# Late gates in the places of k, q and v, and the heads' outputs split early, in a two-block transformer kernel on one core

## The reference

```python
proj = xn @ w_in[i]
q, k, v, u, gates = jnp.split(proj, splits, axis=-1)
...
q = rope(rmsnorm(q, q_norm_gain[i]), cos, sin)
k = rope(rmsnorm(k, k_norm_gain[i]), cos, sin)
...
o = diff_attention(q, k, v, lam)      # 8 heads of 2 x 64, values of 128: (p0 - lam * p1) @ v
o = rmsnorm(o, subln_gain[i]) * (1.0 - lam_init)
attn_branch = o.reshape(bsz, seq, V_COLS) @ w_attn_proj[i]
s = s5_layer(u, ...)
ssm_branch = s @ w_ssm_proj[i]
g_attn, g_ssm = jnp.split(jax.nn.sigmoid(gates), 2, axis=-1)
h = h + (g_attn * attn_branch + g_ssm * ssm_branch) @ w_out[i]
```

## Time and profile before

| | us |
|---|---|
| median of 3 runs | 1477.43 (1476.66 to 1480.17) |
| the profiled execution, its own time | 1480.89 |
| its span, first to last instruction | 1479.1 |
| PE busy | 1414.4 (96%) |
| ACT busy | 829.7 (56%) |
| DVE busy | 658.1 (44%) |
| POOL busy | 203.6 (14%) |
| mean granted clock of PE | 0.988 |

### The profile page before, as it was taken

The page is one execution under the profiler, slowest core; times in us unless marked ns, Lnnn a source line. Parts: engine busy times, 40 slices in busy tenths (PEclk is TensorE's granted clock), DMA queues, the critical chain, the costliest instruction groups (busy, mean ns, idle before and its releaser), DMA issues.

```text
span 1479.1 us, 18389 instructions
## 1 busy us (share of the span) xinstructions
PE 1414.4 (96%) x6786; PEld 1120.0 (76%) x6786; DVE 658.1 (44%) x1153; ACT 829.7 (56%) x1159; POOL 203.6 (14%) x235
## 2 busy tenths in 40 slices
PE   3999999999899999999999999899999999999994
PEld 2887777677578878888888877677788888888883
DVE  4884345465533445555135154746555211212124
ACT  4644666676564566565455376555766655535431
POOL 0120110010011111111111111110111111111111
PEclk9999999999999999999999999999999999999997
DMA  8889876556359878888978997554576888887971
GB/s 256 192 177 185 206 163 145 130 125 150 93 116 245 194 172 198 188 190 192 217 167 196 216 227 172 128 140 113 130 173 141 191 198 188 197 204 176 205 151 57
DMA packets 80675, 255.34 MB, mean 173 GB/s; under 512 B 16592, under 2 KB 17744, under 8 KB 80464
## 3 DMA queue, kind: packets, MB, share of 16 engines
q0 software_dynamic: 32544, 118.50, 44.3%
q1 hardware_dynamic: 47616, 132.57, 29.4%
q10 hardware_dynamic: 432, 3.15, 0.6%
HBM read 128.09 MB, written 3.41 MB: 89 GB/s over the span
## 4 chain that ended last, share of the span: by engine, by line
PE 88%; DVE 4%; ACT 4%; DMA 2%; issue 1%; SPq 1%; POOLq 0%; POOL 0%; DVEq 0%; ACTq 0%
PE pg L500 26%; PE pg L502 25%; PE pg L501 25%; PE ps L637 2%; PE py L701 1%; DMA toep<-k_dram 1%; PE ps L799 1%; PE px L654 1%; PE ps L809 1%; DMA w_lo<-w_raw 1%; DMA w_raw<-weights 1%; PE px L532 1%; PE py L819 1%; ACT w_lo L901 0%; PE px L534 0%
## 5 line engine op out<-in xcount | busy, mean ns | idle before, releaser
L500 PE MATMUL pg<-x_hi,w_hi 128*128 128x512 f32 x1168 | 469.0, 402 | 10.7 <-DVE x_lo L1319 9.9
L502 PE MATMUL pg<-x_hi,w_lo 128*128 128x512 f32 x1168 | 457.8, 392 | 0.0
L501 PE MATMUL pg<-x_lo,w_hi 128*128 128x512 f32 x1168 | 457.6, 392 | 0.0
L468 POOL DMA_DIRECT2D w_lo<-w_raw x226 | 194.8, 862 | 1235.4 <-ACT w_lo L901 1209.1
L900 ACT ACTIVATE w_hi<-w_raw 128x1024 fp32r<-128x1024 f32 x226 | 237.6, 1051 | 123.8 <-PE pg L502 107.1
L500 PEld LDWEIGHTS pg<-x_hi,w_hi 128*128 128x128 f32 x1168 | 221.3, 189 | 64.2 <-issue 13.8
L501 PEld LDWEIGHTS pg<-x_lo,w_hi 128*128 128x128 f32 x1168 | 221.3, 189 | 47.5 <-issue 3.4
L502 PEld LDWEIGHTS pg<-x_hi,w_lo 128*128 128x128 f32 x1168 | 220.9, 189 | 47.2
L901 ACT ACTIVATE w_lo<-w_raw 128x1024 fp32r<-128x1024 f32 x226 | 236.4, 1046 | 0.0
L500 PE MATMUL pg<-act_hi,w_hi 128*128 128x512 f32 x432 | 168.0, 389 | 0.0
L501 PE MATMUL pg<-act_lo,w_hi 128*128 128x512 f32 x432 | 168.0, 389 | 0.0
(11 more groups left out here) (278 smaller groups left out, 1523.3 us busy)
## 6 DMA issues: line engine op xcount, KB each, us to landing
w_raw<-weights SPq DMA_DIRECT2D x226, 512.0 KB, 4.6
w_lo<-w_raw POOLq DMA_DIRECT2D x226, 512.0 KB, 5.7
kq_rot<-kq_raw SPq DMA_DIRECT2D x64, 64.0 KB, 2.4
hid<-x SPq DMA_DIRECT2D x4, 512.0 KB, 5.7
hid<-x ACTq DMA_DIRECT2D x1, 2048.0 KB, 11.0
out<-hid SPq DMA_DIRECT2D x8, 256.0 KB, 2.0
u_dram<-hid SPq DMA_DIRECT2D x4, 256.0 KB, 7.0
pairs<-u_dram SPq DMA_DIRECT2D x8, 128.0 KB, 7.4
```

The lines of the kernel that those rows point to most:

```text
L468: pool.dma_start(w_lo[:, s], w_raw[:, s], accum_op=ALU.add).then_inc(lo_in[s], 16)
L500: pe.matmul(bank[:], wh, xh(k), start=n == 0, stop=False)
L501: pe.matmul(bank[:], wh, xl(k), start=False, stop=False)
L502: last = pe.matmul(bank[:], wl, xh(k), start=False, stop=n == len(ks) - 1)
```

## The change

The late gates move: in iteration 8 gate 4 takes the place of k, gate 5 that of q, gate 6 that of v; in iteration 9 gate 7 takes that of k. Their order, and so the order of the weight units, is unchanged. On ACT each `late_gate` moves with its tile; it is also the call that splits the weights three units on.

The heads' outputs no longer go to `x_hi` and `x_lo`. A new buffer `o_split` of 15 tiles lies over the buffers of rope, k, q and v, a sixteenth tile `pairs_r[:, 2]` over `sqr[:, 0]`; each head gets two of these that no longer hold anything in use. `o_high` (ACT) and `o_low` (DVE) split heads 0 and 1 in iteration 8 behind `turned`, 2 to 4 at its end, 5 and 6 in iteration 9 ahead of the reads of pv 7, and 7 behind the loop. The sum of squares of head 7 (`o_sums`) moves from the end of iteration 9 into attn 0, ahead of its step k = 2. Attn reads the new buffers. `mix_hi` and half of `mix_lo` move on to the buffers of values and probabilities, the other half to that of `y5`.

```diff
@@ -196,6 +196,8 @@
         hid = sb("hid", [P, KT, T])
+        with ExitStack() as s:
+            pairs_r = sb("pairs_r", [P, 4, T], F32R, scope=s)
         pairs = sb("pairs", [P, 4, T])
@@ -214,6 +216,8 @@
             gates = sb("gates", [P, 16, T], scope=first)
+            with ExitStack() as s:
+                mix_lo_high = sb("mix_lo_high", [P, 4, T], F32R, scope=s)
             y5 = sb("y5", [P, SSM_T, T], scope=first)
@@ -241,8 +245,9 @@
                 pt = sb("pt", [P, QB, T], scope=s)
+            o_split = sb("o_split", [P, 15, T], F32R, scope=first)
             mix_hi = sb("mix_hi", [P, KT, T], F32R, scope=first)
-            mix_lo = sb("mix_lo", [P, KT, T], F32R, scope=first)
+            mix_lo_low = sb("mix_lo_low", [P, 4, T], F32R, scope=first)
@@ -301,6 +306,18 @@
         k_dram = nc.dram_tensor("k_dram", (2 * LANE_T, GRP, P), F32).ap()
+        o_last = pairs_r[:, 2]
+        o_slots = [0, 1, 2, 3, 4, 5, 7, 8, 9, 14, 10, 11, 12, 13, 6, None]
+        def o_half(h, low):
+            slot = o_slots[2 * h + low]
+            return o_last if slot is None else o_split[:, slot]
+        def mix_lo(m):
+            return mix_lo_low[:, m] if m < 4 else mix_lo_high[:, m - 4]
@@ -647,6 +664,12 @@
+            def o_sums(h):
+                y_use(("ssq_o", h))
+                pe.wait_ge(o_sq, h + 1)
+                pe.matmul(py[:], ones, kq_sq[2], start=True, stop=True).then_inc(py_full, 1)
             def kq_sums(h, name, n):
@@ -677,6 +700,10 @@
                     named(("k", h), XH, XL)
+                elif h == HEADS:
+                    named(("gate", 4), XH, XL)
+                else:
+                    named(("gate", 7), XH, XL)
                 if h >= 2:
@@ -688,10 +715,6 @@
                     scores(g, 1)
-                if h == HEADS:
-                    named(("gate", 4), XH, XL)
-                if h == HEADS + 1:
-                    named(("gate", 6), XH, XL)
                 if h >= 2:
@@ -703,17 +726,15 @@
                     named(("q", h), XH, XL)
-                if h == HEADS + 1:
-                    named(("gate", 7), XH, XL)
+                elif h == HEADS:
+                    named(("gate", 5), XH, XL)
                 if attends:
...
                     kq_sums(h, "k", 0)
-                if h >= 2:
-                    y_use(("ssq_o", h - 2))
-                    pe.wait_ge(o_sq, h - 1)
-                    pe.matmul(py[:], ones, kq_sq[2], start=True, stop=True).then_inc(py_full, 1)
+                if 2 <= h <= HEADS:
+                    o_sums(h - 2)
                 if attends:
@@ -721,14 +742,17 @@
                 if h == HEADS:
-                    named(("gate", 5), XH, XL)
+                    named(("gate", 6), XH, XL)
+            def last_sums(k):
+                if k == 2:
+                    o_sums(HEADS - 1)
             for m in range(KT):
-                named(("attn", m), XH, XL, first_split=SPLIT["o"] if m == 0 else None)
-            MH, ML = model(mix_hi, mix_lo)
+                named(("attn", m), lambda k: o_half(k, 0), lambda k: o_half(k, 1), first_split=SPLIT["o"] if m == 0 else None,
+                      ahead_of=last_sums if m == 0 else None)
             for m in range(KT):
-                named(("out", m), MH, ML, first_split=SPLIT["mix"] if m == 0 else None)
+                named(("out", m), lambda k: mix_hi[:, k], mix_lo, first_split=SPLIT["mix"] if m == 0 else None)
             statistic(2)
@@ -1085,12 +1109,21 @@
             head_root(("ssq_q", 0), 1, C_EPS64, 1.0, rs_q)
+            def o_high(h):
+                if h == 0:
+                    act.wait_ge(roped, 2 * HEADS)
+                act.wait_ge(o_done, h + 1)
+                put(act.activation(o_half(h, 0), hid[:, h], ACT.Copy), xhi_done)
             for h in range(1, HEADS + 2):
...
                     kq_out(h, "k", 0, "kg")
+                else:
+                    late_gate(4 if h == HEADS else 7)
                 if h >= 2:
@@ -1098,10 +1131,10 @@
                     exps1(g, 1)
-                if h == HEADS:
-                    late_gate(4)
                 if h == HEADS + 1:
-                    late_gate(6)
+                    act.wait_ge(maxed, EXPS[("s", HEADS - 1, QB - 1)] + 1)
+                    for o in (5, 6):
+                        o_high(o)
                 if h >= 2:
@@ -1109,10 +1142,13 @@
                     kq_out(h, "q", 1, "qg")
-                if h == HEADS + 1:
-                    late_gate(7)
+                if h == HEADS:
+                    late_gate(5)
                 if attends:
                     turned(g, 0)
+                if h == HEADS:
+                    for o in range(2):
+                        o_high(o)
                 if h < HEADS:
@@ -1128,11 +1164,11 @@
                 if h == HEADS:
-                    late_gate(5)
-            for h in range(HEADS):
-                act.wait_ge(o_done, h + 1)
-                put(act.activation(x_hi[:, h], hid[:, h], ACT.Copy), xhi_done)
+                    for o in range(2, 5):
+                        o_high(o)
+                    late_gate(6)
+            o_high(HEADS - 1)
             for g in GATES_LAST:
@@ -1603,6 +1639,9 @@
+            def o_low(h):
+                split_lo(SPLIT["o"] + h, o_half(h, 1), hid[:, h], o_half(h, 0))
             def rope_step(h, name, n, ready, dst):
@@ -1635,6 +1674,12 @@
                     turned(g, 1)
+                if h == HEADS:
+                    for o in range(2):
+                        o_low(o)
+                if h == HEADS + 1:
+                    for o in (5, 6):
+                        o_low(o)
                 if h >= 2:
@@ -1649,9 +1694,11 @@
                     rope_step(h, "q", 1, rs_q, qq)
-            for h in range(HEADS):
-                split_lo(SPLIT["o"] + h, x_lo[:, h], hid[:, h], x_hi[:, h])
+                if h == HEADS:
+                    for o in range(2, 5):
+                        o_low(o)
+            o_low(HEADS - 1)
             for m in range(KT + 1):
@@ -1660,7 +1707,7 @@
                 if m > 0:
-                    split_lo(SPLIT["mix"] + m - 1, mix_lo[:, m - 1], mix(m - 1), mix_hi[:, m - 1])
+                    split_lo(SPLIT["mix"] + m - 1, mix_lo(m - 1), mix(m - 1), mix_hi[:, m - 1])
             dve.wait_ge(x2_landed, 16)
...
                 free(tt_(hid[:, m], hid[:, m], done(("out", m)), ALU.add), ("out", m))
```

## The result

| | before | after |
|---|---|---|
| median, us | 1480.17 (1476.66 to 1481.71, 5 runs) | 1471.08 (1470.19 to 1472.54, 5 runs) |
| ratio, 95% interval | | 0.9944 (0.9927 to 0.9962) |
| the profiled execution, own time | 1480.89 | 1472.54 |
| its span | 1479.1 | 1470.7 |
| mean granted clock | 0.988 | 0.991 |

The change is faster by 8.3 us (5.6 to 10.8). Forecast were 11.8 us and 1465.6 us; the measured median lies 0.3 us above the range. A second measurement gave 0.9946 (0.9933 to 0.9960), medians 1471.73 and 1479.61.

The account below looks back on a forecast made before the run. PE bounds the kernel; its waits, drains and slow clock from 383 to 436 us cost about 13.8 us. Attn 0's end moving from 435.5 to 423.7 gains 11.8 us: 1477.43 becomes 1465.6 us, range 1463.5 to 1470.8.

Parts of the forecast that it names:

- the step on the weights: Attn 3's weight load, due at +17.7 us, may take 6.5; median landing 5.7 costs nothing, far end 5.4 us.
- Rival 3: Attn 3 waits for its weights if landing exceeds 6.5 us: up to 5.4 us, 1466 to 1471; chance 0.05.
- the clock's bound: Longest new PE wait, 1.0 us ahead of pv 7, leaves full clock; other end a slow attn 0, +2.9 us.
- the base: The gain was taken off the shown runs' median, 1477.43 us, 3.5 us below the profiled execution.
- Rival 1: Before's slow clock is not in every execution: gain 9.6 us (1467.8) or 6.7 us (1470.7); chance 0.13.
- Rivals 2 and 4: Clock falls at pv 7's new wait, +2.9 us, 0.06; weight loads of 11.9 us make it slower, 1487 us, 0.02.
- Rival 5: The change doesn't do what it says: a queue holds an early split, the stall moves, 1477 us; chance 0.02.

Follow-up runs that it names:

- the halves: Kernel before with only the four late gates moved, 1475.01 us; the change with gates and head 7's sum of squares put back, 1474.99 us.
- the variants without the wait: Changed kernel with the reload of x two tiles later, 1469.10 us; with the sigmoids behind attn 4's weight split, 1469.55 us; with both, 1469.09 us.

## Why the prediction was right and wrong

**Right: the places and sizes in the region itself.** With 0.76 us taken off, turn(7,0) stands at 398.1 (forecast 398.15), gate 6 at 401.6 (401.9), turn(7,2) at 412.6 (413.0), pv 7 at 414.5 (414.9), attn 0 at 416.6 (417.0), its last matmul at 423.6 (423.7). The early splits cost nothing, as said. The granted clock was 1.00 from 380 to 430. Without the collision the whole stretch comes to the 11.8 us: 126.01, 125.90 and 126.15 us in three kernels against 137.85 - 11.8 = 126.05. That it agrees to a tenth is in part luck: attn 0's slow clock, 2.9 us in the profile that I worked from, was 1.6 and 2.7 us in the two further profiles with before's order, whose stretches took 137.51 and 137.14.

**Wrong: the step on the weights.** It followed attn 3's load alone, and that rightly: POOL's issue was forecast 11.2 us behind the start of attn 0, and came at 428.61 - 417.36 = 11.25. It then let everything from attn 1 on "keep its order". The order is kept, but not the distances. ACT came late out of head 7's chain and the sigmoids: it began the split of the first mixture tile at 428.22, though DVE had finished the tile at 426.31. It caught up with two weight splits in a row, and attn 4's load went out with a lead of 9.9 us instead of 11.7 and with the reload of x 0.9 us behind it instead of 2.7. The reload stood in no term of my sum, and the cost of everything from attn 1 on was put at nothing without a price for it: it was 3.8 us in the first profile, 2.2 in the second (1.9 of waiting and 0.3 around it, without the slow clock). What I checked was the engine's queue, not what the queue's DMAs would meet. The far end that I had set, 11.9 us of landing, was what attn 4 got, but I priced it for attn 3 and gave it 0.05. Rival 3 was thus right in kind and wrong in its tile.

**Wrong with it: the clock's bound.** The longest new wait was 1.9 us, not 1.0, and lay beyond the 1.67 us that had done no harm. It cost 1.6 us in one profile and nothing in another.

**Wrong: the base.** The forecast hung on a median of three runs, 1477.43. With five runs it is 1480.17, and 1479.5 to 1480.0 in three further measurements: 2.7 us above it. 1465.6 + 2.7 = 1468.3, and with the 2.2 to 3.8 us of attn 4 it is 1470.5 to 1472.1; measured were 1471.1 and 1471.7. Either error alone would have left the time within the range. The profiled time of 1480.9 lay nearer to these later medians than the median of three; I had seen the 3.5 us between them and read them as the profile's own.

**Wrong: a reading of the profile's page.** I wrote that the slices of the granted clock dip nowhere but in the region of the change and at the ends. They don't dip there either: all slices but the last show 9, since one is 37 us long. The falls show only in the short windows, from which the sum was made, so nothing in it changes; but another fall elsewhere, such as that at 930 us, is hidden in the slices in the same way.

**Rival 1** (the clock's falls are not in every execution) was not borne out as far as profiles show. Both falls are in all three profiles with before's order, that of the kernel before and of the two with its reload moved. Attn 0 took 8.21, 6.92 and 7.98 us in them, so the second fall varied by more than a microsecond in its price, but was never missing. These three executions took 1480.0 to 1481.3 us; none of the fast ones, down to 1476.7, was profiled, so whether those lack a fall stays open. The section of the Trainium skill that the prediction draws on there (TensorE: Matmul & The Clock Gate, "What's actually happening") speaks of the slow matmuls at a kernel's start; that it would hold in mid-kernel was my own step. **Rivals 2 and 4**: no fall behind the wait for `pt` in any profile, and no lasting shortage of weights. **Rival 5**: the halves show that each part does what it says.

**What stays open.** In the medians the variants without the wait gain 2.2 to 2.6 us on the changed kernel of the same measurement, and 10.1 to 10.5 on before, while their stretches gain 11.7 to 12.0 on before's profile. The difference lies within the intervals; upstream of the change, a wait for `toep` was 0.3 us in before's profile and 1.6 to 1.8 in theirs, and none in some other kernels, and the stretch of before was itself 0.3 to 0.7 us shorter in the two further profiles. So part of it is scatter. I did not separate it further.

## What to carry to other kernels

When a step is pulled ahead, follow the DMA issues of every queue that it passes, and write down for each load how long ahead of its use it is issued and what else is issued within its flight; an order that is unchanged says nothing of these distances. A load whose lead is only just longer than its slowest landing in the trace is a term of the sum as soon as the lead shrinks, to be priced at that landing. And take the base of a forecast from more than three runs where the expected gain is below 1%.

## What the runs showed of the hardware

**The DMA that ACT issues went out ahead of ACT's work.** In the code the reload stands behind the weight split of attn 5. In the trace of after it was issued at 431.94 (the row above), ahead of it:

```profile
432.36 1.04 ACT L924 ACTIVATE w_hi<-w_raw 128x1024 fp32r<-128x1024 f32 x1
```

The queue had reached the DMA while the split was still to be executed. With the reload one tile sooner it was more: issued at 425.58, while the weight split of attn 4, which stands before it in the code, began at 427.55. So the place in the code did not give the time of this load, and my forecast of 428.2 for it was 2.6 us late.

**A large load doubled the time of a smaller one that it met.** I took the loads of `w_lo` (512 KB, accumulating, from POOL's queue) around the 2 MB reload in all twelve profiles. The last one issued ahead of the reload took 4.8 to 6.4 us in eight profiles, with the reload 2.0 to 2.8 us behind it, and 5.9 in one, with the reload 1.6 us behind; that is hardly more than the 4.6 to 5.9 us of attn 3's and attn 4's loads that did not meet it. With the reload 0.9 us behind, it took 11.9 us, in both profiles of the changed kernel. The first one issued behind the reload, by 1.8 to 3.2 us, took 9.7 to 12.0 us in every profile, before and after; what differed was the lead. Somewhere between 0.9 and 1.6 us lies the edge, a sharper one than I had thought of; which part of the load is through by then I did not test. Nor is the reload all that lengthens a load: in before one issued at 456.69, when the reload had landed, took 9.5 us. The Trainium skill (DMA: Bandwidth & Descriptors, "SWDGE vs HWDGE vs iDMA") says that a DMA engine goes round between its inner queues, which the two kinds of issuers feed separately. The doubling fits that; no run here shows the queues themselves.

**The clock behind equal waits.** Each of the twelve profiles has the same wait of PE for `v_raw`, 2.82 to 2.83 us, far behind the change. The clock fell behind it in seven of them, to 0.50 to 0.9 in the windows of five us that follow, and not at all in five. In the changed kernel, 925 to 930 us, and in the one with the reload two tiles later:

```profile
925.00:930.00 5.00, 5.00 (x17) 3.97 (x16) 4.83 (x6) 2.63 (x4) 0.86 (x1) 0.66 0.94 189
```

```profile
920.00:925.00 5.00, 3.83 (x19) 3.27 (x20) 4.83 (x6) 4.27 (x7) 0.37 (x1) 1.00 0.98 218
925.00:930.00 5.00, 5.00 (x29) 3.56 (x28) 4.46 (x5) 0.00 (x0) 0.49 (x1) 1.00 0.91 210
```

The latter's wait ended at 921.17, the former's at 924.54. The wait of 1.9 us at attn 4 had a fall in one of two profiles, the wait of 2.7 us at attn 3 in its only one, and the waits of 1.67 us ahead of the statistic in none of twelve. So the price of a wait of 2 to 3 us is the wait, and sometimes 1.6 us or more on top: some of the scatter of a kernel's runs, and nothing to explain a difference of one profile by. The Trainium skill (TensorE: Matmul & The Clock Gate, "What's actually happening") has the number of slow matmuls at a kernel's start vary between runs of one kernel. These profiles show the like in mid-kernel: the two of the changed kernel differ behind the same wait at attn 4, and over all kernels there are twelve equal waits with seven falls.
